# Normalizing and gating two attention branches' probabilities per head on GpSimd, instead of their outputs by a turned factor tile

## The reference

```python
# selected (SLC) and window (WIN) branch, keys and values shared by 4 heads each
p = masked_softmax(s, valid)
o_slc = einsum('bsgqk,bkgd->bsgqd', p, v)          # the same for o_win
g = sigmoid(gates.reshape(B, S, KH, G, 3))
o = g[..., 0:1] * o_cmp + g[..., 1:2] * o_slc + g[..., 2:3] * o_win
...
# top-k branch (DSA): softmax over the 128 keys that an index score chose; no gate of its own
o_a = einsum('bthk,btkd->bthd', p, v)
merged = sigmoid(gate_a) * (o_a @ w_up_a) + sigmoid(gate_b) * (o_b @ w_up_b)
```

## Time and profile before

| | |
|---|---|
| median of 3 runs | 739.38 us (739.08 to 739.41) |
| profiled execution | 739.83 us, of it 738.1 us span |
| PE, PEld busy | 731.2 us, 651.5 us |
| DVE, ACT, POOL busy | 583.5, 437.4, 178.2 us |
| granted PE clock | 0.999 over the span |

### The profile page before, as it was taken

The page is one execution under the profiler, slowest core; times in us unless marked ns, Lnnn a source line. Parts: engine busy times, 40 slices in busy tenths (PEclk is TensorE's granted clock), DMA queues, the critical chain, the costliest instruction groups (busy, mean ns, idle before and its releaser), DMA issues.

```text
span 738.1 us, 12691 instructions
## 1 busy us (share of the span) xinstructions
PE 731.2 (99%) x4686; PEld 651.5 (88%) x4686; DVE 583.5 (79%) x1079; ACT 437.4 (59%) x803; POOL 178.2 (24%) x192
## 2 busy tenths in 40 slices
PE   9999999999999999999999999999999999999998
PEld 9998987877997778777888899999999888799997
DVE  5478888779986877766667989888887788897987
ACT  7768487756677887654356555566556544533341
POOL 3110337424555544300012422222230000000000
PEclk9999999999999999999999999999999999999999
DMA  9621222102111121103533233333442333324342
GB/s 344 244 81 46 80 87 80 36 29 58 58 58 58 29 62 54 57 31 96 194 110 113 88 115 115 89 106 93 115 115 87 107 94 90 109 88 115 115 123 78
DMA packets 22861, 71.00 MB, mean 96 GB/s; under 512 B 2448, under 2 KB 5648, under 8 KB 22544
## 3 DMA queue, kind: packets, MB, share of 16 engines
q1 hardware_dynamic: 22656, 69.97, 30.5%
q10 hardware_dynamic: 144, 0.22, 0.1%
HBM read 68.08 MB, written 2.10 MB: 95 GB/s over the span
## 4 chain that ended last, share of the span: by engine, by line
PE 84%; DVE 8%; ACT 3%; issue 2%; DMA 1%; POOL 1%; DVEq 0%; SPq 0%; POOLq 0%
PE psum L2148 23%; PE psum L2150 23%; PE psum L2149 23%; PE psum L2156 5%; PE psum L2345 4%; PE psum L2322 2%; PE psum L2323 2%; DVE w_lo L1486 2%; DMA x2T<-in_xT 1%; ACT w_hi L1060 1%; POOL nrstd L958 1%; DVE cmp_in L1618 1%; DVE q_st L1642 1%; ACT h L1060 1%; DVE x2T L1853 1%
## 5 line engine op out<-in xcount | busy, mean ns | idle before, releaser
L1060 ACT ACTIVATE w_hi<-stage 128x512 fp32r<-128x512 f32 (+4 forms) x149 | 114.7, 778 | 32.0 <-PE psum L2150 26.8
L2148 PE MATMUL psum<-hT_hi,w_hi 128*128 128x256 f32 (+1 forms) x324 | 113.5, 350 | 0.3 <-DVE w_lo L1889 0.3
L2149 PE MATMUL psum<-hT_lo,w_hi 128*128 128x256 f32 (+1 forms) x324 | 107.3, 331 | 0.0
L2150 PE MATMUL psum<-hT_hi,w_lo 128*128 128x512 f32 (+1 forms) x264 | 90.6, 343 | 0.0
L1486 DVE TENSOR_TENSOR w_lo<-stage,w_hi 128x1024 fp32r<-128x1024 f32 (+4 forms) x58 | 56.7, 984 | 41.4 <-ACT w_hi L1060 37.2
L1060 ACT ACTIVATE w_hi<-s_sum 128x1024 fp32r<-128x1024 f32 x46 | 48.8, 1060 | 54.2 <-PE psum L2150 51.9
L2149 PE MATMUL psum<-a_lo,w_hi 128*128 128x512 f32 (+1 forms) x224 | 77.0, 344 | 0.0
L1248 ACT ACTIVATE prob<-prob,neg_max 128x128 f32<-128x128 f32 (+3 forms) x96 | 53.8, 560 | 32.1 <-DVE neg_max L1700 31.4
L1021 POOL TENSOR_TENSOR w_lo<-stage,w_hi 128x512 fp32r<-128x512 f32 x46 | 59.5, 1298 | 36.1 <-ACT w_hi L1060 36.1
L2149 PE MATMUL psum<-t_lo,w_hi 128*128 128x256 f32 x240 | 67.9, 283 | 0.0
L2148 PE MATMUL psum<-t_hi,w_hi 128*128 128x256 f32 x240 | 67.9, 283 | 0.0
(11 more groups left out here) (316 smaller groups left out, 2041.5 us busy)
## 6 DMA issues: line engine op xcount, KB each, us to landing
stage<-in_panels SPq DMA_DIRECT2D x104, 512.0 KB, 3.5
xT_in<-in_xT SPq DMA_DIRECT2D x8, 260.0 KB, 4.7
x_in<-in_x SPq DMA_DIRECT2D x4, 512.0 KB, 7.4
phi<-in_phi SPq DMA_DIRECT2D x2, 1024.0 KB, 6.3
x2T<-in_xT SPq DMA_DIRECT2D x1, 2048.0 KB, 9.0
stage<-in_panels SPq DMA_DIRECT2D x4, 408.0 KB, 3.2
stage<-in_panels SPq DMA_DIRECT2D x4, 384.0 KB, 4.3
stage<-in_panels SPq DMA_DIRECT2D x7, 212.0 KB, 4.9
```

The costliest lines, as they stand in the source:

```text
L1060: return nc.scalar.activation(dst, src, ACT.Copy, scale=scale)
L2148: mm(dst, a_h, b_h, start=start, stop=False)
L2149: mm(dst, a_h, b_l, start=False, stop=False)
L2150: return mm(dst, a_l, b_h, start=False, stop=stop)
```

## The change

For WIN and DSA there are no `inv`, `fac` and `close` with a factor. In their place stands a step `weigh` for every unit, listed right behind the `qk` of the next unit: DVE inverts the unit's row sum (for WIN it also multiplies by the gate, a second instruction on one value per partition), and GpSimd multiplies the unit's probabilities, 128 x w, in place by that one value per row. PE's `pT` waits for GpSimd's product instead of ACT's exponential. WIN's `close` is then only the addition to `o_b`; DSA has no `close` and no `o_a`: `oT_hi` and `oT_low` read the O bank itself, and `oT_low` releases it. The places of `oT_hi` of the first three DSA tiles move from units 85, 95, 96 to 85, 88, 93. SLC keeps its factors. The diff, cut:

```diff
-OB_PLACES, OA_PLACES = (70, 80, 81, 82), (85, 95, 96)
+OB_PLACES, OA_PLACES = (70, 80, 81, 82), (85, 88, 93)
...
+    WEIGHED = WIN
...
     for ti in range(NU // H):
-        at_unit(ti * H + 9, "inv", ti, at=early)
-        at_unit(ti * H + 10, "fac", ti)
+        if ti // TT < WEIGHED:
+            at_unit(ti * H + 9, "inv", ti, at=early)
+            at_unit(ti * H + 10, "fac", ti)
...
         if u < NU:
             step("qk", u)
+        if 1 <= u <= NU and units[u - 1][0] >= WEIGHED:
+            step("weigh", u - 1)
...
-        if u >= TAKEN_AT and (u - TAKEN_AT) % H == 0:
+        if u >= TAKEN_AT and (u - TAKEN_AT) % H == 0 and (u - TAKEN_AT) // H < DSA * TT:
             step("close", (u - TAKEN_AT) // H)
...
-    step("close", NU // H - 1)
     step("oT_hi", 0, TT - 1)
...
-        def out_tile(m, tt):
-
-            return (o_b[:, tt, :, :], tt) if m else (o_a[:, tt % 2, :, :], TT + tt)
+        def out_tile(eng, m, tt):
+
+            if m:
+                return o_b[:, tt, :, :], tt
+            ps = wait_full(eng, ("O", DSA * TT + tt))
+            return ps.rearrange("p (k t) -> p k t", k=4), TT + tt
...
# SyncE, before the reload of x for the residual
-            sp.wait_ge(oT_lo_done, 2 * TT)
+            for tt in (TT - 2, TT - 1):
+                wait_drained(sp, ("O", DSA * TT + tt))
...
# GpSimd
+                elif kind == "weigh":
+                    u0, = a
+                    w = (units[u0][1] + 1) * P
+                    pool.wait_ge(unit_inv, u0 - WEIGHED * TT * H + 1)
+                    prob = probs[u0 % PROBS][:, 0:w]
+                    nc.gpsimd.tensor_tensor(prob, prob, row_inv[:, u0:u0 + 1].to_broadcast([P, w]), ALU.mult)\
+                        .then_inc(weighed, 1)
...
# VectorE
+                elif kind == "weigh":
+                    u, = a
+                    br, tt, h = units[u]
+                    ve.wait_ge(exp_done, u + 1)
+                    inv = row_inv[:, u:u + 1]
+                    if br == WIN:
+                        link(nc.vector.reciprocal(inv, row_sum[:, u:u + 1]))
+                        tt_op(inv, inv, gates[:, tt, h:h + 1, 1 + WIN], ALU.mult).then_inc(unit_inv, 1)
+                    else:
+                        nc.vector.reciprocal(inv, row_sum[:, u:u + 1]).then_inc(unit_inv, 1)
...
                     if br == WIN:
-                        link(tt_op(ps, ps, fac[:, :, :], ALU.mult))
+                        if br < WEIGHED:
+                            link(tt_op(ps, ps, fac[:, :, :], ALU.mult))
                         o = o_b[:, tt, :, :]
                         ins = tt_op(o, o, ps, ALU.add)
                     else:
-                        o = out_tile(br != DSA, tt)[0]
-                        if br == DSA and tt >= 2:
-                            ve.wait_ge(oT_lo_done, TT + tt - 1)
-                        ins = tt_op(o, ps, fac[:, :, :], ALU.mult)
+                        ins = tt_op(o_b[:, tt, :, :], ps, fac[:, :, :], ALU.mult)
...
# TensorE
                 elif kind == "pT":
                     u, = a
-                    te.wait_ge(exp_done, u + 1)
+                    if units[u][0] >= WEIGHED:
+                        te.wait_ge(weighed, u - WEIGHED * TT * H + 1)
+                    else:
+                        te.wait_ge(exp_done, u + 1)
```

More of the change, by code:

```diff
@@ L551, in hybrid_layer @@
         relu = place("relu", [P, RELUS, S], Z + 59 * K)
-        o_a = place("o_a", [P, 2, 4, P], Z + 43 * K)
         cmp_e = place("cmp_e", [P, TT, H, CP], Z + 47 * K)
@@ L641, in hybrid_layer @@
         inv_done = sem("inv_done")
+        unit_inv = sem("unit_inv")
+        weighed = sem("weighed")
         fac_spread = sem("fac_spread")
@@ L1272, in _ @@
                     m, tt = a
-                    src, n = out_tile(m, tt)
+                    src, n = out_tile(se, m, tt)
                     if m:
@@ L1277, in _ @@
                         wait_drained(se, ("cmpO", tt))
+                        wait_drained(se, ("O", TT + tt))
                     else:
                         se.wait_ge(oT_lo_done, TT)
-                    wait_drained(se, ("O", TT * (1 if m else 2) + tt))
                     copy(oT_hi[m][:, :, tt * P:(tt + 1) * P], src).then_inc(oT_hi_done, 1)
@@ L1795, in _ @@
                     br, tt, _ = units[ti * H]
-                    wait_drained(ve, ("fac", ti))
+                    if br < WEIGHED:
+                        wait_drained(ve, ("fac", ti))
                     ps = wait_full(ve, ("O", ti)).rearrange("p (k t) -> p k t", k=4)
                     if br == WIN:
-                        link(tt_op(ps, ps, fac[:, :, :], ALU.mult))
+                        if br < WEIGHED:
+                            link(tt_op(ps, ps, fac[:, :, :], ALU.mult))
                         o = o_b[:, tt, :, :]
@@ L1810, in _ @@
                     m, tt = a
-                    src, n = out_tile(m, tt)
+                    src, n = out_tile(ve, m, tt)
                     ve.wait_ge(oT_hi_done, n + 1)
                     tok = slice(tt * P, (tt + 1) * P)
-                    tt_op(oT_lo[m][:, :, tok], src, oT_hi[m][:, :, tok].bitcast(F32), ALU.subtract)\
-                        .then_inc(oT_lo_done, 1)
+                    ins = tt_op(oT_lo[m][:, :, tok], src, oT_hi[m][:, :, tok].bitcast(F32), ALU.subtract)
+                    if m:
+                        ins.then_inc(oT_lo_done, 1)
+                    else:
+                        drained(ins, ("O", DSA * TT + tt))
                 elif kind == "split" and a[0] not in pool_panels:
@@ L2406, in _ @@
                     if what == "up" and i == 0 and k == 0:
-                        te.wait_ge(oT_lo_done, TT if m else 2 * TT)
+                        if m:
+                            te.wait_ge(oT_lo_done, TT)
+                        else:
+                            for tt in (TT - 2, TT - 1):
+                                wait_drained(te, ("O", DSA * TT + tt))
                     dst = open_bank(("tile", t)) if k == 0 else psum[:, bank[("tile", t)][0], :]
```

## The result

| | before | after |
|---|---|---|
| median of 6 runs each, us | 739.6 (739.08 to 740.22) | 745.14 (744.18 to 745.48) |
| ratio after/before, 95% interval | | 1.0073 (1.0063 to 1.0084) |
| profiled span, us | 738.1 | 743.6 |

The account below looks back on a forecast made before the run. PE's own instructions were taken to bound the kernel. -3.5 (blocks) - 0.4 (end of chain) + 3.45 (GpSimd) + 2.7 (DVE in WIN) = +2.25 us, giving 741.6 us on the median 739.38, range 736.6 to 745.0.

Parts of the forecast that it names:

- 32 blocks, 3.5 us, "firm": On PE, 32 of 48 factor blocks go, at 0.109 us each: 3.5 us off, called a firm number.
- the whole 3.9: Gain from the removed blocks (3.5 us) and the vanished wait before the last up tile (0.4 us).
- PE has no gap for them: Reason given that the removed blocks' time is fully gained: PE has no idle time to hide them.
- The end of the chain, -0.4: Before the merged branch's last up tile, PE's 0.40 us wait goes, since ACT starts about 0.7 us sooner without DSA's close.
- Behind it nothing else is late: After the last up tile, no further wait was expected; PE's tiles are next.
- GpSimd, +3.45: PE waits for GpSimd's products: group 3 0.54, units 59 0.48, 67 0.70, 76 0.40, 79 0.89, 90 0.44 us.
- Group 3: SLC factor behind unit 32's weighing, where PE already waits: +0.54 us from DVE's pair and one GpSimd product.
- DVE in WIN, +2.7, and 0 behind 207.6 us: Inversion and gate product, 0.33 us plus 0.2 hold per unit, delay unit 48's scores 2.7 us; later about even, 0.
- 2.45 + 0.87: DVE's room in the first stretch: 2.45 us spare, and unit 46 drained 0.87 us before unit 48's scores.
- Rival 3: Every WIN gate product meets a running GpSimd instruction: 5.3 in place of 2.7, 744.2 us, up to 745.5; chance 0.11.
- What would show it: Signs: 16 blocks, some 3 us PE idle by the scores' drain, gate product mean near 0.37, no last up tile wait.
- GpSimd about 2x slower: Skill page's advice against the move: a 512 product would cost 1.38 us instead of 1.17, giving 742.6.

Follow-up runs that it names:

- no_weigh: The changed kernel without both weigh steps, DVE's and GpSimd's, so WIN and DSA stay undivided and ungated: 736.94 us, ratio 0.9963 to the kernel before.
- pool_only: The changed kernel without DVE's weigh; GpSimd multiplies each unit by a gate column already there, nothing is divided: 738.92 us, ratio 0.9990 to the kernel before.
- no_gate: The changed kernel with DVE's inversion alone in WIN, its product with the gate left out, GpSimd's product kept: 739.89 us, ratio 1.0005 to the kernel before.

## Why the prediction was right in sign and short by 3.5 us

- **32 blocks, 3.5 us, "firm".** The price was right, what it leaves was not. PE's blocks went from 48 to 16, and each group of four gave 0.36 to 0.44 us where it stood, but `no_weigh` kept 2.75 us of the whole 3.9. 0.6 us went to waits for copies that the blocks had covered, 1.2 to the wait behind the reload of x. "PE has no gap for them" was the wrong reason: a block that other engines use to catch up is no pure cost. In the whole change the second took less (0.83 before the MLP pair, against 1.70); why isn't shown.
- **The end of the chain, -0.4.** Right. No wait before the last up tile; the stretch behind unit 95 is 0.75 us shorter, 0.84 by the sum. "Behind it nothing else is late" failed: the reload and the first MLP pair are.
- **GpSimd, +3.45.** Right in kind and about right in size. Its products took 46.7 us against 48. PE waited at unit 67 (0.78 us against 0.70) and 79 (0.65 against 0.89), and 0.61 us near unit 61 for the turning of a query, which the profile puts down to DVE's `q_st` (0.48 had been set for unit 59); at 59 and 76 PE was late by 0.22 and 0.14 only (0.48 and 0.40 forecast), at 90 not at all. Two places that weren't walked were late by GpSimd instead: units 42 and 45, 0.30 and 0.50. The DSA stretch came out at +0.53 against +0.69. Alone, without DVE's part, the products cost 2.0 us (`pool_only`), 0.9 of them by holding DVE's chain on `cmp_e`, for which the forecast had no term. Group 3 is the exception: +1.17 against +0.54, since the bank's drain behind the held gate product wasn't walked.
- **DVE in WIN, +2.7, and 0 behind 207.6 us.** The second is the step that failed. The mechanism was right, and so was the hold (0.19 us each against 0.2): without the gate product nothing is lost (`no_gate`), with it 5.2 us are, of which 3.2 are holds. Up to the scores of unit 48 PE came 3.25 us later, by the forecast's terms 2.80. That this comes so near is in part luck: the wait that the forecast named, at those scores, is 0.49 us. The rest lies at results that PE takes from DVE earlier: group 3's factor, which had no slack at all, and the first turning of `cmp_e`, which had 1.38 us and not 2.45 + 0.87, with ACT's copy behind it. Behind 207.6 us the forecast set 0 for DVE and 0.48 for unit 59, and PE lost 2.9 us: 0.50 at unit 45, 0.93 at the second turning of `cmp_e`, 0.22 at unit 59, 0.61 at a query, the rest in smaller pieces. The forecast's own numbers make the error plainer. 10.1 less 2.7 is 7.4 us of new work against 10.4 of spare time, so not "about even" but 3 us of room, and with holds of 0.4 us it is 0.8 too much, not 3. DVE had that room on the average of the window and still came late at the results that PE waits for.
- **Rival 3.** Its time (744.2 to 745.5) is the one measured, its mechanism isn't: by it every gate product would be held, by 0.4 us on average. Nineteen of 32 weren't, and the mean hold is 0.19. Its upper end, 745.5, took in part of the 3 us behind 207.6 us that its own numbers give as 0.8.
- **What would show it.** Blocks, maximum, mean and the missing wait were as written. PE's idle time in the first stretch (2.8 us) came with other releasers than the scores' drain: that appears once, just behind that stretch (0.49 us at 211.14); the rest is `cmp_e` and ACT's copy of it, the factor and GpSimd.
- **GpSimd about 2x slower.** The GPSIMD Engine Reference of the Trainium skill, section 4.1, would have made a 512 product 1.38 us. The trace has 1.041, 1.5 times the 0.69 that the forecast doubled: the page's factor is too high for a product with one value per row. With two full operands, 1.298 us, it is nearly right.

## What to carry to other kernels

An engine's spare time in a window is no slack: it counts only up to the first result that the bounding engine takes from its queue. Walk those results one by one, and take the smallest room. A step taken off the bounding engine may have been another engine's time to catch up; look at the next wait behind it, and at the next transfer that starts sooner for it. And a small DVE product of two SBUF tensors beside a GpSimd at work on wide rows should be priced with the rest of GpSimd's running instruction (here 0.19 us on the mean, 1.0 at most), or written with one tensor. New GpSimd work holds the DVE products that are there already, too.

## What the runs showed of the hardware

A DVE product of one value per row, 0.16 us, took up to 1.154 us beside GpSimd, and each of the thirteen long ones ends with the GpSimd instruction that was running (178.76 + 0.78 with 178.49 + 1.04). The reduce that stood in for it, with one input, took 0.153 to 0.156 us in all 32 places. The page SBUF — State Buffer of the Trainium skill, section SBUF: two separate sides, states this as an exclusive lock on a port pair that a VectorE instruction takes when it has two SBUF inputs; the trace agrees in these thirteen places, down to instructions of 128 values. In the seven beside GpSimd's power of four values per row, which also reads SBUF, it does not: there the product took its 0.16 us. Less expected: 32 such instructions, 0.16 us of work each, cost 5.2 us of a kernel of 740 (745.14 against 739.89 without them).
